# A two-block transformer kernel: one projection's operand and weights ahead of the shared norm's root, ten low weight halves on GpSimd

## What is computed

```python
def rms_norm_2(x, g):
    y = x * lax.rsqrt(jnp.mean(x * x, axis=-1, keepdims=True) + EPS)
    return y * g

for l in range(2):
    hn = rms_norm_2(h, norm_mix_pre[l])
    mkv = rms_norm_2(mem, mem_norm) @ w_mem_kv[l]        # 256 memory rows
    if l == 0:
        proj = hn @ w_in_a                               # lru, gate, memory queries
        y = rg_lru(conv(proj[:, :768])) * gelu(gate)
    else:
        proj = hn @ w_in_b                               # 12 query heads, memory queries
        y = sliding_window_attention_with_sinks(rope(q), shared_k, shared_v, sinks)
    m_out = memory_attention(mq, mk, mv)                 # 4 heads over the memory
    h = h + rms_norm_2(concat(y, m_out) @ w_out[l], norm_mix_post[l])
    f = swiglu_ffn(rms_norm_2(h, norm_ffn_pre[l]), w_ffn_in[l], w_ffn_out[l])
    h = h + rms_norm_2(f, norm_ffn_post[l])
    if l == 0:
        kv = rms_norm_2(h, norm_kv) @ w_kv_shared        # shared_k (rope), shared_v
```

## Time and profile before

| what | us |
|---|---|
| median of 3 runs | 1850.1 |
| lowest, highest | 1843.49, 1850.68 |
| the profiled execution | 1849.64 |
| its span in the trace | 1847.5 |
| TensorE (PE) busy | 1770.6 (96%) |
| TensorE's weight loads (PEld) busy | 1564.9 (85%) |
| VectorE (DVE) busy | 1206.7 (65%) |
| ScalarE (ACT) busy | 879.0 (48%) |
| GpSimd (POOL) busy | 145.1 (8%) |
| mean granted TensorE clock | 0.983 of 2.4 GHz |

### The profile page before, as it was taken

One profiled execution on the slowest core, in us unless ns is written; L12 is line 12 of the kernel. 1 busy time (PEld: TensorE's weight loads), 2 busy tenths in 40 slices (PEclk: granted clock), 3 DMA queues, 4 the chain that ended last, 5 costly groups with the idle time before them and its releaser, 6 DMA issues.

```text
span 1847.5 us, 39145 instructions
## 1 busy us (share of the span) xinstructions
PE 1770.6 (96%) x15536; PEld 1564.9 (85%) x15536; DVE 1206.7 (65%) x1953; ACT 879.0 (48%) x1466; POOL 145.1 (8%) x133
## 2 busy tenths in 40 slices
PE   7999989999999999998999999999999998999997
PEld 5884677888888878877888999999899997789997
DVE  4787864885687675534566775577576557757653
ACT  4436634532243235555445664467644454464443
POOL 0002002000000100024431000100100000010000
PEclk9999989999999999999999999999999999899999
DMA  8763014365455424210005555534365554036553
GB/s 332 257 225 125 2 47 148 116 190 172 159 170 173 146 95 137 92 36 4 4 21 170 159 181 187 186 130 138 121 199 182 178 163 137 1 112 204 183 172 104
DMA packets 71184, 256.70 MB, mean 139 GB/s; under 512 B 7568, under 2 KB 11536, under 8 KB 69904
## 3 DMA queue, kind: packets, MB, share of 16 engines
q1 hardware_dynamic: 71056, 254.87, 41.9%
HBM read 253.79 MB, written 1.05 MB: 138 GB/s over the span
## 4 chain that ended last, share of the span: by engine, by line
PE 87%; DVE 6%; ACT 4%; issue 2%; DMA 1%; SPq 0%; POOL 0%; DVEq 0%; ACTq 0%; POOLq 0%
PE bank L389 24%; PE bank L390 23%; PE bank L391 23%; PE bank L381 2%; PE bank L2131 1%; ACT weights_hi L329 1%; DMA arena<-ada_w 1%; PE bank L1103 1%; PE bank L2156 1%; PE bank L2136 1%; DVE weights_lo L336 1%; PE bank L408 1%; PE bank L1088 1%; PE bank L2930 1%; DVE a L2429 1%
## 5 line engine op out<-in xcount | busy, mean ns | idle before, releaser
L389 PE MATMUL bank<-x_hi,weights_hi 128*128 128x256 f32 (+1 forms) x2008 | 638.3, 318 | 24.3 <-DVE x_lo L427 6.1
L390 PE MATMUL bank<-x_lo,weights_hi 128*128 128x256 f32 (+1 forms) x2008 | 628.8, 313 | 0.0
L391 PE MATMUL bank<-x_hi,weights_lo 128*128 128x256 f32 (+1 forms) x2008 | 628.7, 313 | 0.0
L336 DVE TENSOR_TENSOR weights_lo<-ring,weights_hi 128x1024 fp32r<-128x1024 f32 x374 | 459.0, 1229 | 225.2 <-ACT weights_hi L329 222.1
L329 ACT ACTIVATE weights_hi<-ring 128x1024 fp32r<-128x1024 f32 x374 | 393.4, 1055 | 397.5 <-PE bank L391 397.4
L389 PEld LDWEIGHTS bank<-x_hi,weights_hi 128*128 128x128 f32 x2008 | 385.9, 192 | 58.1 <-issue 24.4
L390 PEld LDWEIGHTS bank<-x_lo,weights_hi 128*128 128x128 f32 x2008 | 386.1, 192 | 22.6 <-issue 1.9
L391 PEld LDWEIGHTS bank<-x_hi,weights_lo 128*128 128x128 f32 x2008 | 386.0, 192 | 21.5
L389 PE MATMUL bank<-hidden_hi,weights_hi 128*128 128x256 f32 (+1 forms) x864 | 271.6, 314 | 0.0
L390 PE MATMUL bank<-hidden_lo,weights_hi 128*128 128x256 f32 (+1 forms) x864 | 271.6, 314 | 0.0
L391 PE MATMUL bank<-hidden_hi,weights_lo 128*128 128x256 f32 (+1 forms) x864 | 271.6, 314 | 0.0
(11 more groups left out here) (391 smaller groups left out, 2183.3 us busy)
## 6 DMA issues: line engine op xcount, KB each, us to landing
ring<-mlp_w SPq DMA_DIRECT2D x128, 512.0 KB, 4.3
ring<-w_ffn_in SPq DMA_DIRECT2D x88, 512.0 KB, 3.3
a<-ada_t SPq DMA_DIRECT2D x32, 512.0 KB, 3.6
mix<-ada_t SPq DMA_DIRECT2D x32, 512.0 KB, 4.3
ring<-w_ffn_out SPq DMA_DIRECT2D x32, 512.0 KB, 3.5
ring<-gdn_w_in SPq DMA_DIRECT2D x24, 512.0 KB, 3.3
ring<-even_w_in SPq DMA_DIRECT2D x18, 512.0 KB, 5.0
tables<-ada_t SPq DMA_DIRECT2D x16, 512.0 KB, 4.2
```

Of the source, the lines that this page charges most:

```text
L336: nc.vector.tensor_tensor(w_lo[:, g % AHEAD, :], ring[:, g % RAW, :], w_hi[:, g % AHEAD, :].bitcast(F32), ALU.subtract).then_inc(lo_done[g ...
L389: pe.matmul(dst, lhs[0](k), rhs[0](k), start=start and k == 0, stop=False)
L390: pe.matmul(dst, lhs[0](k), rhs[1](k), start=False, stop=False)
L391: last = pe.matmul(dst, lhs[1](k), rhs[0](k), start=False, stop=stop and k == nk - 1)
```

## The change

1. The shared norm. ScalarE makes all eight high blocks of in_b's operand, then in_b's first high weight half, then the strips' copy (split off from `act_root` as `act_strips`), then the second high weight half, then the root. VectorE makes all eight low blocks and in_b's first two low weight halves before it waits for the root. High halves 2 and 3 of in_b stay behind the root.
2. Attention A. The low halves of six tiles (the last two of mem_blocks[1], the first four of out_a) go from VectorE to GpSimd, which takes them ahead of its sums for out_a's norm (`split_lo_pool`).
3. Attention B. The low halves of out_b's first four tiles go from VectorE to GpSimd, ahead of its copies of the sinks.

```diff
--- before.py
+++ after.py
@@ -336,6 +336,11 @@
             nc.vector.tensor_tensor(w_lo[:, g % AHEAD, :], ring[:, g % RAW, :], w_hi[:, g % AHEAD, :].bitcast(F32),
                                     ALU.subtract).then_inc(lo_done[g % AHEAD].sem, 1)
 
+        def split_lo_pool(pool, g):
+            pool.wait_ge(hi_done[g % AHEAD].sem, g // AHEAD + 1)
+            nc.gpsimd.tensor_tensor(w_lo[:, g % AHEAD, :], ring[:, g % RAW, :], w_hi[:, g % AHEAD, :].bitcast(F32),
+                                    ALU.subtract).then_inc(lo_done[g % AHEAD].sem, 1)
+
         def follow(eng, split, tiles):
 
             for t in range(tiles.n):
@@ -523,9 +528,13 @@
                 pe.wait_ge(strips_copied.sem, self.copied + 1)
                 pe.matmul(BSUM[:, 0:self.w], ones, strip_sums, start=True, stop=True).then_inc(sums_done.sem, 1)
 
-            def act_root(self, act):
+            def act_strips(self, act):
                 act.wait_ge(sums_done.sem, self.added + 2)
                 nc.scalar.activation(strip_sums, BSUM[:, LAT:T], ACT.Copy, scale=1.0 / 32).then_inc(strips_copied.sem, 1)
+
+            def act_root(self, act, strips=True):
+                if strips:
+                    self.act_strips(act)
                 super().act_root(act)
 
         strips_copied = sig("strips_copied")
@@ -3162,8 +3171,12 @@
             return bank[4 + g % 4][:, 0:LAT]
 
         def pool_second(pool):
+            for g in range(mem_blocks[1].tiles.first + 2, out_a.tiles.first + AHEAD):
+                split_lo_pool(pool, g)
             for x in (post_a, ffn_a.post):
                 x.norm.pool_add(pool)
+            for t in range(AHEAD):
+                split_lo_pool(pool, out_b.tiles.first + t)
             pool.wait_ge(B["small"].sem, 4)
             att_b.pool(pool)
             for x in (post_b, ffn_b.post):
@@ -3337,14 +3350,16 @@
             post_a.act(act)
             ffn_a.act(act, post_a)
             ffn_a.post.act_next(act, pre_kv)
-            for k in range(KB // 2):
+            for k in range(KB):
                 pre_b.act(act, k)
-            pre_kv.norm.act_root(act)
-            for k in range(KB // 2, KB):
-                pre_b.act(act, k)
+            kv_sh.ahead(act, 0)
+            pre_kv.norm.act_strips(act)
+            kv_sh.ahead(act, 1)
+            pre_kv.norm.act_root(act, False)
             for n in range(4):
-                kv_sh.ahead(act, n)
-                if n < 2:
+                if n >= 2:
+                    kv_sh.ahead(act, n)
+                else:
                     act.wait_ge(evac_dve.sem, kv_sh.lin.base + n + 1)
                     for x in range(2):
                         nc.scalar.activation(shk[half(1 - x), 2 + n, :], shk[half(x), n, :], ACT.Copy).then_inc(B["swapped"].sem, 1)
@@ -3430,39 +3445,33 @@
             recurrence(4)
             recurrence(5)
             mem_att_a.dve_max(dve, 0)
-            for t in range(2, 4):
-                split_lo(dve, mem_blocks[0].tiles.first + t + AHEAD)
             recurrence(6)
             mem_att_a.dve_max(dve, 1)
             mem_att_a.dve_max(dve, 2)
             mem_att_a.dve_probs(dve, 0)
-            for t in range(2):
-                split_lo(dve, mem_blocks[1].tiles.first + t + AHEAD)
             for k in range(LB):
                 out_x[0].dve(dve, k)
                 if k == 2:
                     mem_att_a.dve_probs(dve, 1)
             mem_att_a.dve_probs(dve, 2)
             mem_att_a.dve_max(dve, 3)
-            split_lo(dve, mem_blocks[1].tiles.first + 2 + AHEAD)
             mem_att_a.dve_probs(dve, 3)
             mem_att_a.dve_out(dve, 0)
             mem_att_a.dve_out(dve, 1)
-            split_lo(dve, mem_blocks[1].tiles.first + 3 + AHEAD)
             mem_att_a.dve_out(dve, 2)
             mem_att_a.dve_out(dve, 3)
             for k in range(LB, KB):
                 out_x[0].dve(dve, k)
             post_a.dve(dve, ffn_a.pre)
             ffn_a.dve(dve, pre_kv)
-            for k in range(KB // 2):
+            for k in range(KB):
                 pre_b.dve(dve, k)
+            for n in range(2):
+                split_lo(dve, kv_sh.tiles.first + n + AHEAD)
             pre_kv.norm.wait(dve)
             for n in range(4):
                 if n < 2:
                     kv_sh.dve_scaled(dve, n, shk[:, n, :], rstd[:, 0:LAT])
-                    for k in (4 + 2 * n, 5 + 2 * n):
-                        pre_b.dve(dve, k)
                 else:
                     if n == 2:
                         dve.wait_ge(B["kv_turned"].sem, 1)
@@ -3470,13 +3479,14 @@
                     dve.wait_ge(block_done.sem, kv_sh.done(n))
                     nc.vector.tensor_scalar(shv[:, n - 2, :], kv_sh.lin.bank(n)[:, 0:LAT], root_t[:, 2 * (n - 2):2 * (n - 2) + 1], None,
                                             ALU.mult).then_inc(evac_dve.sem, 1)
-                split_lo(dve, kv_sh.tiles.first + n + AHEAD)
+                    split_lo(dve, kv_sh.tiles.first + n + AHEAD)
             for t in range(in_b.tiles.n):
                 in_b.dve_scaled(dve, t, qs[:, t - 2, :] if t >= 2 else mq[:, t, :], rstd[:, 0:LAT])
                 if t == 2:
                     for i in range(3):
                         att_b.dve_max(dve, i)
-                split_lo(dve, in_b.tiles.first + t + AHEAD)
+                if t + AHEAD < in_b.tiles.n:
+                    split_lo(dve, in_b.tiles.first + t + AHEAD)
                 if t == 4:
                     att_b.dve_probs(dve, 0)
                     att_b.dve_probs(dve, 1)
```

## The result

| | before | after |
|---|---|---|
| median, lowest to highest of 20 runs | 1848.6, 1843.3 to 1852.5 | 1853.5, 1846.3 to 1862.3 |
| ratio after to before, 95% interval | | 1.0035 (1.0023 to 1.0048) |
| profiled execution, its span | 1849.64, 1847.5 | 1851.37, 1849.2 |

The change makes the kernel slower by 4.8 us by the medians and 6.5 by the ratio, which is within 0.5%. The forecast was +4.9 us and 1854.5 us, with a range of 1844 to 1861. One execution of the kernel before on the last of them took 8169.65 us and is in none of the ratios.

What follows compares the result with a forecast made beforehand. TensorE was taken as the bound, busy 1770.6 of 1847.5 us, leaving its gaps and low-clock stretches. Norm -3.6, attention A +6.0 and +2.0 for the clock, attention B +0.5: +4.9 us, 1854.5 us, range 1844 to 1861.

Steps and rivals of the forecast that it cites:

- norm: gap and clock: Shared norm: w_in_b starts 2.1 us earlier and 1.5 us of low clock goes, -3.6 us in all.
- new wait for the strips' copy: Shared norm: the copy queues behind a high half on ScalarE, so TensorE's summing matmuls start 0.65 us later.
- a GpSimd low half: Attention A: one low half of 1024 columns takes GpSimd 2.33 us, scaled from its operations over two full operands.
- a hold of VectorE: Attention A: each GpSimd low half holds VectorE work on two SBUF operands for 2.15 us; PSUM-reading work goes on.
- last maximum of attention A late by: Attention A: VectorE's last maximum ends 6.3 us late, 12.9 of holds less 4.6 of removed work and 2.0 of overlap.
- w_out's start late by: Behind attention A: TensorE's first stream of w_out, which hangs on the last maximum, starts 6.0 us late.
- clock behind it: Behind attention A: TensorE's clock falls because it works only part of the time, costing 2.0 us (0 to 3.0).
- attention B: Four GpSimd low halves make VectorE's third rotation, for which TensorE waits, 0.5 us late (-1.5 to +2.0).
- rival (d): Shared norm: part 1 doesn't keep the clock up, 1.5 us less won, 1856.0 us; shares the forecast's 0.6 chance.
- rival (a): The engines don't exclude each other for these operations, VectorE is only relieved: -4.6 us, 1845.0 us; chance 0.13.
- Rival (b): Exclusion, but GpSimd low halves of 1.64 us: +2.0 at attention A, no clock fall, 1848.0 us; chance 0.15.
- Rival (c): Low clock lasts 15 us over w_out's stream behind attention A: 7.5 instead of 2.0, 1860.0 us; chance 0.12.

Runs made afterwards that it cites:

- norm_clock: The kernel before with eleven idle matmuls in TensorE's wait ahead of w_in_b at the shared norm: 1846.2 us, ratio 0.9991 to the kernel before.
- p1_norm_only: The kernel before with the reordering at the shared norm alone, all low weight halves on VectorE: 1843.6 us, ratio 0.9987 to the kernel before.
- p1_again: The kernel before with the reordering at the shared norm alone, run once more on another chip: 1842.2 us, ratio 0.9976 to the kernel before.
- p2_attn_a_only: The kernel before with only the six low halves around attention A moved from VectorE to GpSimd: 1855.3 us, ratio 1.0048 to the kernel before.
- p2_no_hold: The kernel before with attention A's six low halves on GpSimd, each cut to 8 of 1024 columns, same waits and signals: 1846.3 us, ratio 0.9999.

## Why the forecast held, point by point

| step | forecast | measured | where |
|---|---|---|---|
| norm: gap and clock | -3.6 | -3.8 | -4.43 + 0.67 |
| new wait for the strips' copy | 0.65 | 0.67 | 2.65 - 1.98; 0.41 of it idle |
| a GpSimd low half | 2.33 | 2.34 to 2.79, median 2.41 | L341 |
| a hold of VectorE | 2.15 | 2.16 | scans 5.75 against 3.59 |
| last maximum of attention A late by | 6.3 | 6.8 | 24.35 against 17.54 after the first scan |
| w_out's start late by | 6.0 | 7.4 | 27.85 against 20.48 |
| clock behind it | 2.0 | 1.6 | 8.93 - 7.37 |
| attention B | +0.5 | +0.51 | third rotation's scores |
| sum | +4.9 | +5.7 | -3.8 + 8.9 + 0.5 by landmarks, rounded |
| whole kernel | +4.9 | +4.8 (medians), +6.5 (ratio) | |

The prediction was right in its mechanism. That it meets the medians within 0.1 us is luck: the landmarks give 0.8 more, the ratio 1.6 more, and part 3 measured alone came out with the other sign.

**Part 1** went as worked out. w_in_b started 0.63 us after the turning began, and TensorE has no gap there that a weight's low half ends. The clock stayed up, so rival (d) falls, and `norm_clock` prices the clock by itself at 1.4 us, where I had taken 1.5. Of the parts' runs, `p1_norm_only` and `p1_again` give -2.4 and -4.4 us (by 0.9987 and 0.9976 of some 1848), on both sides of -3.8.

**Part 2** was right in its mechanism, and its sum was too small by 0.9 us (8.9 by landmarks against 6.0 + 2.0 = 8.0; in `p2_attn_a_only` 9.2). The ledger can be read off the rows of after. The six subtractions hold six operations ahead of the last maximum: 2.16 + 1.30 + 1.53 + 2.09 + 2.14 + 2.14 = 11.4 us. Less four low halves, 4.6, that is 6.8, and the maximum is 6.8 late. I had 12.9 - 4.6 - 2.0 = 6.3: the overlap with maxima was 1.5 and not 2.0, because the negation right behind a maximum, 128x2 with one operand and a constant, is held too (1.47 us, and 1.70 at 1278.81), which I had ruled out by letting only products of two SBUF operands be held. The second miss is the step from the maximum to w_out. I had taken 0.3 off; it became 0.6 longer (3.50 us against 2.94), with the turning and mixing products ahead of w_out at half clock already, 1.97 us against 1.09 for a mixing. Part of the clock's price thus fell ahead of w_out's start, and what fell behind it was less than my 2.0. `p2_no_hold` takes the long subtractions away and the loss is gone: rival (a), that there is no exclusion, falls, and with it its gain of 1 us from relief, which measured 0. Rival (b)'s short length of 1.64 us falls by the L341 row.

The Trainium skill, SBUF — State Buffer, section "SBUF: two separate sides", says that the shared pair of ports is locked for a whole instruction against VectorE work with two SBUF inputs or in a mode that uses both ports. The prediction weighed only the first half of that for the scans, and they are held, 5.75 us against 3.59. The small negation speaks for the second half; the Trainium skill, VectorE: DVE Perf Modes, section "The perf-mode tier table (the rule you actually need)", has tensor_scalar over SBUF in float32 in such a faster mode. It does not list the reciprocal, so the one that was not held here neither supports nor contradicts it.

**Rival (c)**, 15 us at half clock behind attention A, did not happen: w_out's steps are 0.21 us apart to 1298.97, for 3.4 us. The prediction's sign for it, a low clock that runs on for over 10 us, was there all the same, so that sign was badly chosen: counted from the first slow product, the turning at 1287.39, to 1298.97 the clock is low for 11.6 us. TensorE idles for 2.2 of them and waits there for VectorE and ScalarE, not for its clock, and what counts for (c) is the dense stream, which lost 1.6 us and not 7.5. I had put the danger in the wrong place, though. A stretch of that length exists at attention B, and I took it as a constant of the kernel. It differs by profile: 34.2, 31.2, 30.0 or 28.1 us to the last sink copy. The profiled pair differs by +1.7 us, where the medians differ by +4.8, with -6.0 there and +3.0 ahead of attention A, which nothing ties to the change. The parts alone, -3.4 (mean of the two runs of part 1) + 8.9 (part 2, by its ratio) - 2.2 (part 3), come to +3.3; the ratio of the whole is +6.5 with 2.3 either way. Each part has some 2 to 3 us either way of its own, so the two sums don't contradict each other, and they don't confirm more than the size either. For part 3 the sign stays open: its work comes 0.5 to 0.7 us later in every profile that has it, and its time came out 2.2 us better, with an interval that ends at no change. Either the low-clock stretch is more often short with it, which two profiles in favour (28.08 and 28.17) and one against (34.11) can't tell, or it is scatter.

**The prediction's signs of being right** were all there: the stream within 0.3 us of the turning's end, clock 1.00, subtractions that start 2.67, 2.36 and 2.30 us apart where they queue, low halves of the operand at 3.23 us and scans at 5.75, a gap of 3.22 us.

## What to carry to other kernels

Before giving an elementwise operation of two SBUF operands to GpSimd, count it against VectorE: it is relieved of 1.14 us and held for 2.2 us, unless it is idle or reads PSUM in that time; if the move has to be made, cut the operation into short pieces (+2.7 us instead of +9.2 here, in one execution each). Making operands and the first weights ahead of a reduction's root uses time in which the engines were idle; it cost 0.67 us here, for the copy that came to stand behind a high half, and its gain is the wait plus the clock behind the wait. Before booking a difference of two profiles to a change, cut both by landmarks and look at the lines that the change can't touch: here the stretch ahead of the first scan, the same code in fourteen kernels, differed by up to 8.8 us. A wait of 2 us on TensorE in the midst of short products can be worth filling with matmuls of no use (3.5 us for one line at attention B, by a ratio with 0.6 to 6.5), but where dense work follows the gain is no more than a filling that is too long takes back (`norm_clock`).

## What the runs showed of the hardware that I had not expected

- VectorE's multiplication by a constant of 128x2 is held like a wide product beside a GpSimd subtraction (1.47 and 1.70 us, alone 0.17), and a 128x2 reciprocal isn't (0.15, at 1566.16 inside GpSimd's 1565.84 to 1568.24).
- The hold goes with the length of one GpSimd instruction: 2.16 us beside 128x1024, 0.5 beside 128x256, both at the scans. The hold works the other way too: pieces of 256 columns take GpSimd 0.72 to 0.75 us where nothing is in their way, as its additions of that size do, others 0.84 to 1.19, and the one issued at 1272.17, beside VectorE's product over 128x1536 (1272.15, 1.75 us), took 2.32.
- The granted clock of one stretch is no constant of its code. Behind attention B's wait it was 0.50 for 17, 10 or 7 us in kernels with the code of before at that place, and for 17 or 3 us in those with part 3; with TensorE kept busy through the wait it was 1.00 in all three kernels. The stretch is worth 1.6 to 7.5 us (28.08 less 26.49, 34.17 less 26.67), as much as the change as a whole. Whether it differs between executions of one kernel isn't shown: the kernel profiled twice had 7 us both times. That kernel's mean granted clock, like any other's, does differ by execution, 0.983 to 0.991 over its 24 runs, without a record of where. The Trainium skill, TensorE: Matmul & The Clock Gate, section "What's actually happening", says that the same kernel shows a different count of slow matmuls at its start from run to run.
